# Seven half-width products instead of eight in 27 of 66 gate/up pairs, their weight sums made by adding transfers

## The reference

```python
FFN_DIM = D_FF = 2816                     # 22 features of 128
def conv_ffn(x, ln_g, up_w, conv_w, conv_b, down_w):          # blocks s = 0 and 1
    u = causal_dwconv(rms_norm(x, ln_g) @ up_w, conv_w, conv_b)     # three taps along the sequence
    gate, up = u[..., :FFN_DIM], u[..., FFN_DIM:]
    return (jax.nn.silu(gate) * up) @ down_w
def swiglu(xn, w_gate, w_up, w_down):                         # block s = 2
    return (jax.nn.silu(xn @ w_gate) * (xn @ w_up)) @ w_down
```

## Time and profile before

| | |
|---|---|
| median of 3 runs | 2398.46 us (2397.93 to 2400.35) |
| the profiled execution | 2399.27 us, span 2397.5 us |
| TensorE busy | 2371.2 us of the span |
| VectorE, ScalarE, GpSimd busy | 1484.8, 1086.1, 357.9 us |
| granted TensorE clock, mean | 0.998 |
| third block's gate and up, first to second down projection | about 2044 to 2330 us |
| read from memory | 215.87 MB |

### The profile page before, as it was taken

How to read it: one execution, slowest core, us unless ns; L and a number is a source line. 1 busy time by engine, 2 the same in 40 slices (tenths; PEclk the granted TensorE clock), 3 DMA queues, 4 the chain that set the end, 5 groups by cost and what they waited for, 6 DMA issues and landing times.

```text
span 2397.5 us, 30764 instructions
## 1 busy us (share of the span) xinstructions
PE 2371.2 (99%) x11952; PEld 1944.2 (81%) x11952; DVE 1484.8 (62%) x2356; ACT 1086.1 (45%) x1878; POOL 357.9 (15%) x286
## 2 busy tenths in 40 slices
PE   8999999999999999999999999999999999999999
PEld 6677878888888877788888877787788878898987
DVE  6778776763666777766456547534655445873763
ACT  6654554442445677644234334324443334442433
POOL 0252252210111000122011100001210001100001
PEclk9999999999999999999999999999999999999999
DMA  4532223223223221232332332231234332233232
GB/s 164 109 93 79 80 70 99 97 86 108 97 83 120 75 76 49 73 108 92 93 106 87 91 131 84 71 102 57 72 123 136 115 106 79 81 105 99 95 97 89
DMA packets 74847, 226.24 MB, mean 94 GB/s; under 512 B 8144, under 2 KB 12368, under 8 KB 74576
## 3 DMA queue, kind: packets, MB, share of 16 engines
q1 hardware_dynamic: 70272, 215.90, 28.1%
q10 hardware_dynamic: 4432, 8.39, 2.0%
HBM read 215.87 MB, written 8.39 MB: 94 GB/s over the span
## 4 chain that ended last, share of the span: by engine, by line
PE 60%; DVE 1%; ACT 0%; issue 0%; DMA 0%; POOL 0%; POOLq 0%; DVEq 0%; ACTq 0%; SPq 0%
PE bank L1272 59%; PE bank L1276 1%; DVE t L2230 1%; DVE t L2233 1%; ACT t L1715 0%; DVE t L2241 0%; DMA t<-in_w 0%; POOL t L2877 0%; ACT t L1718 0%; ACT L1718 0%; DVE t L2237 0%; DVE t L2798 0%; POOLq L3100 0%; DVEq L3100 0%; DVE t L2644 0%
## 5 line engine op out<-in xcount | busy, mean ns | idle before, releaser
L1272 PE MATMUL bank<-t 128*128 128x512 f32 (+5 forms) x11526 | 2346.4, 369 | 19.1 <-DVE t L2233 7.9
L1272 PEld LDWEIGHTS bank<-t 128*128 128x128 f32 (+2 forms) x11526 | 1901.0, 186 | 433.3 <-issue 80.1
L1715 ACT ACTIVATE t<-t 128x1024 fp32r<-128x1024 f32 (+5 forms) x676 | 564.0, 847 | 564.6 <-PE bank L1272 276.6
L2230 DVE TENSOR_TENSOR t<-t 128x1024 fp32r<-128x1024 f32 (+7 forms) x774 | 687.3, 901 | 202.9 <-ACT t L1715 192.4
L1718 ACT ACTIVATE t<-t 128x512 f32<-128x512 f32 (+6 forms) x610 | 367.5, 616 | 455.8 <-DVE t L2230 307.1
L2877 POOL TENSOR_TENSOR t<-t 128x512 f32<-128x512 f32 (+4 forms) x206 | 316.3, 1542 | 1551.9 <-ACT t L1718 559.7
L2230 DVE TENSOR_TENSOR t<-bank,t 128x512 f32<-128x512 f32 (+4 forms) x434 | 279.2, 648 | 425.2 <-PE bank L1272 414.7
L2233 DVE SCALAR_TENSOR_TENSOR t<-t 128x512 f32<-128x512 f32 (+5 forms) x536 | 386.6, 733 | 102.3 <-ACT t L1718 63.8
L1715 ACT ACTIVATE t<-bank 128x512 f32<-128x512 f32 (+4 forms) x184 | 84.7, 477 | 205.4 <-PE bank L1276 146.9
L2880 POOL TENSOR_SCALAR t<-t 128x128 f32<-128x128 f32 (+3 forms) x64 | 40.9, 645 | 478.6 <-ACT t L1715 247.6
L2233 DVE SCALAR_TENSOR_TENSOR t<-bank,t 128x512 f32<-128x512 f32 x56 | 38.5, 688 | 68.8 <-PE bank L1272 68.8
(11 more groups left out here) (30 smaller groups left out, 53.0 us busy)
## 6 DMA issues: line engine op xcount, KB each, us to landing
t<-in_w SPq DMA_DIRECT2D x304, 512.0 KB, 3.4
t<-in_w SPq DMA_DIRECT2D x48, 384.0 KB, 3.0
t<-in_w SPq DMA_DIRECT2D x56, 320.0 KB, 3.0
t<-in_w SPq DMA_DIRECT2D x28, 256.0 KB, 2.8
tab<-t ACTq DMA_DIRECT2D x1, 2560.0 KB
t<-in_x SPq DMA_DIRECT2D x8, 256.0 KB, 5.0
t<-tab SPq DMA_DIRECT2D x8, 256.0 KB, 3.7
spill<-t ACTq DMA_DIRECT2D x1, 2048.0 KB, 8.3
```

The costliest lines, as they stand in the source:

```text
L1272: return eng.matmul(out, lhs, rhs, start=start, stop=stop, skip_group_check=loose)
L1715: return eng.activation(out, in_, ACT.Copy, scale=scale)
L2230: return eng.tensor_tensor(out, a, b, o)
```

## The change

- Quads in all three feed-forward blocks: f = 9, 12, 14, 16, 18, 20 in blocks 0 and 1, and f = 4, 6 to 10, 12 to 20 in block 2. There rows of quads follow each other without an ordinary feature between them.
- The order of the products is p1, p5, p6, p3, p7, p2, p4, and the units are other ones: unit 0 (one half only) for p1, unit 1 (s12) for p5 and p6, unit 2 (s34) for p3 and p7, unit 3 for p2 and p4.
- The weights of a quad are one region in memory: gate low, up low, up high, gate high (four chunks of 512 columns each). Of it, SyncE loads a first quarter (256 KB) and the last half (512 KB) into raws, and three quarters (768 KB, `base`) into a buffer `sums`. GpSimd issues two transfers that add to what is there: the second and third quarter of the region onto the first two of `sums` (`add1`, 512 KB), then the first quarter of `sums` onto its third (`add2`, 256 KB). VectorE makes one sum (`add3`, 512 columns) into `sum4`. The four VectorE sums of before are gone.
- There are two `sums` buffers, used in turn; the second lies in the scratch of the norms and of the tees.
- `SUM_AGES` says how many ticks before the quad base, add1, add2 and add3 are issued. s34 is split and cut in two halves, since they lie in two tensors.
- In blocks 0 and 1 the quad's gate and up go through the convolution; its ticks are longer there.
- `cut_age` stays 2 within a quad (before: 1 for one unit).

```diff
-QUADS = (4, 5, 7, 8, 10, 12, 13, 15, 16, 18, 19)
-PRODUCTS = ("p1", "p2", "p6", "p5", "p7", "p3", "p4")
+QUADS = {0: (9, 12, 14, 16, 18, 20), 1: (9, 12, 14, 16, 18, 20), 2: (4, 6, 7, 8, 9, 10, 12, 13, 14, 15, 16, 17, 18, 19, 20)}
+QUAD_LIST = [(s, f) for s in range(3) for f in QUADS[s]]
+SUM_AGES = ((19, 15, 9, 3), (19, 15, 9, 3), (12, 9, 5, 1))
+PRODUCTS = ("p1", "p5", "p6", "p3", "p7", "p2", "p4")
+QUAD_HALF = {"p1": (0, 0), "p5": (1, 0), "p6": (1, 1), "p7": (2, 0), "p3": (2, 1), "p4": (3, 0), "p2": (3, 1)}
...
-        self.loads += [(gate, 0, DC, gate_c + f * P, P), (up, 0, DC, up_c + f * P, P)]
+        region = self.region((gate, 0, 4, gate_c + f * P, P), (up, 0, 4, up_c + f * P, P),
+                             (up, 4, 4, up_c + f * P, P), (gate, 4, 4, gate_c + f * P, P))
+        first = self.load(region, 0, S)
+        last = self.load(region, 2 * S, UNIT)
+        sources = (("raw", first, S), ("s12", (s, f), UNIT), ("s34", (s, f), UNIT), ("raw", last, UNIT))
         for i, product in enumerate(PRODUCTS):
-            if i % 2 == 0:
-                age, self.cut_age = self.cut_age, 1 if i == 4 else self.cut_age
-                u = self.ring(sources[i // 2])
-                self.cut_age = age
-                g.units.append(u)
+            if QUAD_HALF[product][0] == len(g.units):
+                g.units.append(self.ring(sources[len(g.units)]))
...
-        self.start("sum1", f, t - 5)
-        self.start("sum2", f, t - 3)
+        for name, age in zip(("base", "add1", "add2", "add3"), SUM_AGES[s]):
+            self.start(name, (s, f), t - age)
...
     def source(self, u):
+        if kind == "s12":
+            return [(0, n, self.sums(r)[:, S:3 * S])]
+        return [(0, S, self.sums(r)[:, 0:S]), (S, n, self.buf.sum4[:, :])]
...
     # ScalarE, quads: p1 copied at age 1, p5 at 2, p6 at 3 (before: p1 1, p6 3, p5 4); blocks 0 and 1 also:
+        for kind, age in (("ga", 7), ("up", 8)):
+            for s, f in at("quad", T - age):
+                func(ACT.Identity, buf.fv[n % 6][:, :], buf.fu[n % 3][:, 2:S + 2], pc(f"fcb{s}", ft),
+                     pc(f"fcw{s}", 3 * ft)).then_inc(*sig["tap0"].up((kind, s, f)))
...
     # VectorE, quads: bank d (p3) added at age 4, p7 at 5, bank a (p2) and the gate row at 6, the up row at 7
+        for sf in at("add3", T):
+            w.wait_ge(*K.loaded(last))
+            w.wait_ge(*K.added(sf, 1))
+            tt(buf.sum4[:, :], K.sums(sf)[:, 2 * S:3 * S], buf.raws[last % N_W][:, S:UNIT], ADD).then_inc(*sig["sum"].up(sf))
...
     # GpSimd
+    def adds(T):
+        for sf in at("add1", T):
+            w.wait_ge(*K.based(sf))
+            eng.dma_start(K.sums(sf)[:, 0:UNIT], K.region(region)[:, S:3 * S], accum_op=ADD).then_inc(
+                *sig.added[i][0].up())
+        for sf in at("add2", T):
+            w.wait_ge(*K.added(sf, 0))
+            eng.dma_start(K.sums(sf)[:, 2 * S:3 * S], K.sums(sf)[:, 0:S], accum_op=ADD).then_inc(*sig.added[i][1].up())
...
     # SyncE
+    def base(sf):
+        if before:
+            w.wait_ge(*sig["cut"].at(plan.quad_units[before][4]))
+        eng.dma_start(K.sums(sf)[:, 0:3 * S], K.region(region)[:, 0:3 * S]).then_inc(*sig.base[i].up())
```

More of the change, by code:

```diff
@@ L528, in ffn @@
         late = 5 if s < 2 else 2
[L529 to L531 removed]
+        apart = 4 if s == 2 else 12
+        for k in range(4 if QUADS[s] else 0):
+            self.once("tees", (s, k), lambda k=k: self.past("rms", src, 3) and (
+                k == 0 or self.past("tees", (s, k - 1), apart)))
         self.start("ffn", s)
@@ L2530, in quads @@
+        for s, f in at("quad", T - 6):
             vg, _ = K.quad_rows(f)
[L2531 to L2537 removed]
@@ L2551, in quads @@
-        for f in at("quad", T - 10):
-            src, i = h_of(2, f)
-            hi, lo = buf.operand(src, i)
-            w.wait_ge(*sig["hi"].at(src, i))
-            stt(lo, K.quad_rows(f)[1][:, :], -1.0, hi.bitcast(F), MUL, SUB).then_inc(*sig["lo"].up(src, i))
+            row = K.rms_row(FFN_IN[s])
+            w.wait_ge(*full(("gu", s, f, "a")))
+            tt(vg[:, 0:H2], K.of(("gu", s, f, "a"))[:, 0:H2], vg[:, 0:H2], ADD).then_inc(*leave(("gu", s, f, "a")))
+            w.wait_ge(*empty(("rb", FFN_IN[s])))
@@ new lines, in fu_free, with taps @@
+    def fu_free(n, s):
+        if n >= 3:
+            w.wait_ge(*sig["tap"].at(("ga" if (n - 3) % 2 == 0 else "up", s, (n - 3) // 2), 2))
+    def taps(key):
+        kind, s, f = key
+        n = 2 * f + (kind == "up")
+        ft = f + FFC * (kind == "up")
+        v, ub = buf.fv[n % 6], buf.fu[n % 3]
+        for k in (1, 2):
+            w.wait_ge(*(sig["tap0"].at(key) if k == 1 else sig["tap"].at(key, 1)))
+            stt(v[:, :], ub[:, 2 + k:S + 2 + k], pc(f"fcw{s}", 3 * ft + k), v[:, :], MUL, ADD).then_inc(
+                *sig["tap"].up(key, k))
@@ L3042, in sync_program @@
                 load(plan.units[u][1] + N_W)
+        for sf in at("base", T):
+            base(sf)
         for h in at("tb", T):
```

412 lines of the change are left out of this document (242 added, 170 removed).

## The result

The changed kernel takes 2480.8 us, the median of four runs (2478.7 to 2481.6), against 2398.9 for the kernel before, measured beside it: a ratio of 1.034 [1.0322, 1.0357]. It is slower by 82 us, where 17 were forecast. The sign was right; the size was not, and it lies outside the forecast range.

The account below looks back on a forecast made before the run. Bound: TensorE's columns plus its waits. Columns -12.8, old waits -2.8, late cuts (13 + 0.5) + (2.8 + 0.25 + 13.2), adding transfers +3: +17.2 on 2398.46, so 2416 us; range 2388 to 2440, the forecast's own 2408 to 2424.

Parts of the forecast that it names:

- the quad's worth of 0.80 us: TensorE's columns: each quad saves 0.80 us where nothing waits; sixteen more quads give -12.8 us.
- The wait at a joint: Third block, quad behind a quad: p5 waits 1.06, say 1.1 us, for VectorE's cut, twelve times, 13.2 us.
- The wait before p3: Quads behind ordinary features: unit 2's cut late by 1.3 us ten times (blocks 0, 1), 1.4 us twice (third block).
- Those terms: All forecast waits for late cuts, at joints and behind ordinary features or down projections: 29.75 us over 27 quads.
- the adding transfers: Chain base, add1, add2 of each quad: 10.2 to 16.4 us, taken as 13.3; costs 3 us in all.
- 3 us for the three: Third block, f = 4, 6 and 12: sums late by 1.0 us each; 0 at 10.2, 12 at 16.4.
- hidden at 13.3: Rows of quads: base issued 15.1 us ahead, so a 13.3 us chain costs nothing; at 16.4, 0.6 more a quad.
- The lead: Time by which the third block's base is issued ahead: 13.3 us at f = 4, 6, 12; 15.1 us in rows.
- The forecast's own formula, (chain + 7.2) / 2: Time per quad in a row when the chain exceeds its lead; 11.8 us for a 16.4 us chain.
- Rival 3: Adding transfers become the bound in the third block, at 16.4 us a chain: 2432 us; chance 18%.
- some 0.1 us more each time: Unit 2's split and cut, now on two halves instead of one piece, each take some 0.1 us longer.
- GpSimd's own multiplies wait behind its transfers by a few us at most, four ticks before they are needed.: GpSimd's queue: multiplies delayed a few us behind adding transfers, with four ticks to spare; no cost was added.

Follow-up runs that it names:

- e1: The changed kernel without GpSimd's two adding transfers (add1, add2), so its weight sums are wrong: 2430.2 us.
- e8: The changed kernel with the third block's base issued two ticks earlier (14 instead of 12): 2449.7 us.
- e10: The changed kernel without add2, the second adding transfer of each quad; base and add1 stay: 2439.8 us.
- e7: The changed kernel with ten spaced quads in block 2, base 19 ticks ahead, and the multiply before quads of blocks 0 and 1 on VectorE: 2415.4 us.
- e4: The changed kernel with the multiply of the feature ahead of a quad moved from GpSimd to VectorE in blocks 0 and 1: 2465.7 us.
- e3: The changed kernel with quads only in the third block (all 15), none in blocks 0 and 1: 2462.3 us.
- e5: The changed kernel with the old order of products and units, all 27 quads and the adding transfers kept: 2471.5 us.
- e11: Spaced-quad, old-order kernel (2399.8 us) with third-block multiplies before quads on VectorE and p7 waiting only for its half of the cut: 2389.6 us.
- e12: Spaced-quad, old-order kernel (2399.8 us) with the multiply of the feature before a quad on VectorE in the third block too: 2394.6 us.
- e9: Spaced-quad, old-order kernel (2399.8 us) with unit 2's cut a tick earlier, ahead of the taps, and third-block multiplies before quads on VectorE: 2399.1 us.

## Why the prediction was right in sign and wrong in size

**Right, as the runs showed.** The bound (TensorE's columns plus its waits), the quad's worth of 0.80 us and the sum as a method: it closes within 2.5 us in twelve of thirteen kernels. The wait at a joint, forecast 1.06, is 1.08 in e1, e8 and e10, and in those joints of the changed kernel that no transfer holds (0.53 in e7, where add3 stands two ticks earlier). The wait before p3, forecast 1.3 in blocks 0 and 1 and 1.4 in the third, is 1.33 (e4) and 1.2 to 1.4 (e1). f = 12 was put at 0.25 and is 0.21. SyncE issues a row's base at 7.3 us of the quad two before by the forecast, at 7.7 by the trace where that quad did not wait. Those terms came to 29.75 us; the runs have 15.1 (e4, blocks 0 and 1) and 16.1 (e1, third block) for them.

**The step that failed: the adding transfers.** "The chain is 10.2 to 16.4 us; I take the middle, 13.3", and so "3 us for the three" at f = 4, 6 and 12 and "hidden at 13.3" in the rows. Measured, this term is 48 us in the third block (64.3 to 16.1, e1): 21.6 at f = 4, 6 and 12, and 26.6 at the joints. The 15 chains of the third block took 14.5 to 21.3 us, 17.5 on the mean.

The bounds were drawn from plain transfers of the earlier trace rows. The base, put at 4.0, took 4.4 to 7.9 us, 5.1 in the median; add1, 3.4 to 6.8 by the bounds, took 5.1 to 7.2, 5.4 in the median; add2, 2.8 to 5.6 by the bounds, took 3.3 to 7.8, 4.1 in the median. Missing were the 0.3 and 0.5 us from one link's landing to GpSimd's issue of the next. In blocks 0 and 1, where no second chain runs beside the first, the chain took 15.8 us on the mean. So by the means, 2.5 of the missing 4.2 us were the links' own length and the gaps, and 1.7 came with the third block, where in a row of quads the last link of one chain runs beside the first of the next (there the base took 6.0 us on the mean, 5.0 in blocks 0 and 1; add2 took 7.0 to 7.8 at three joints). The lead was wrong too at the starts of two rows: 9.7 us at f = 4 and 11.5 at f = 6 where 13.3 was forecast (13.8 at f = 12). In the rows it was right: 14.8 to 16.0 us at the joints that waited, against 15.1.

A quad that waits long gives the next chain a longer lead, so long and short joints take turns, and the mean spacing from f = 13 to 20 is (2389.46 - 2294.49) / 7 = 13.6 us, where 11.2 was forecast. The forecast's own formula, (chain + 7.2) / 2, gives 12.5 with the 17.7 us that the chains of these eight quads took on the mean. The remaining 1.1 us a quad (the split and cut behind the landing, and the half-clock stretches, are candidates) was not taken apart. Rival 3 had the right mechanism, and a chain too short for its price: 2432.

**A size within a right mechanism: the wait before p3.** 2.4 us, not 1.3, in ten quads: 10.7 us (e4). For a cut in two halves the forecast gave "some 0.1 us more each time". But the multiply comes between the halves, and the second takes 1.07 us more. The cut of the earlier trace rows had been priced with a multiply beside it, and had not suffered, since it was one instruction and came first (2.20 us for the multiply, in the earlier trace rows too).

**A sentence that the traces contradict.** "GpSimd's own multiplies wait behind its transfers by a few us at most, four ticks before they are needed." They are needed sooner. At f = 4 of the changed kernel a multiply left the queue at 2096.16, behind an add1 issued at 2095.50 that had waited for its base. ScalarE's next step came at 2097.81, released by it, and TensorE stood idle 1.15 us before the quad, where e1 has no gap (timelines of GpSimd, ScalarE and TensorE):

```profile
2096.16 1.62 POOL L2972 TENSOR_TENSOR t<-t 128x512 f32<-128x512 f32 x1
...
2097.81 1.15 ACT L1764 ACTIVATE t<-t 128x512 fp32r<-128x512 f32 x2 [8.17 <-POOL t L2972]
...
2099.91 1.67 PE L1314 MATMUL bank<-t 128*128 128x256 f32 x12 [1.15 <-DVE t L2298]
```

In e7 the same cost 5 us at f = 18. The 48 us that e1 took away hold both, the late sums and this.

**A term that was missing: the clock.** The forecast let TensorE wait at full speed. After many of its waits of 2 us and more the granted clock was 0.50 for 3.4 us or longer; the changed kernel's matmuls are busy 26.7 us longer than their columns (2385.1 against 2371.2 - 12.8). Some 9 of that is in blocks 0 and 1 and went with the waits in e4; 14.5 is in the third block and went in e1. The waits of 1.1 to 1.4 us that I had forecast bring none: e1 has no such stretch in the third block, e4 none in blocks 0 and 1.

In the forecast's units: -12.8 - 3.4 + 29.8 (as forecast) + 48 (transfers, with their clock) + 19.5 (multiply, with its clock) = +81.

**Open.** Which of its neighbours makes add2 take 7.8 us instead of 4.1 was not measured; nor why the third block waits 5 to 6 us more when blocks 0 and 1 are quicker or have no quads (e4, e3), nor which of several equal waits brings a half-clock stretch.

## What to carry to other kernels

A chain of dependent transfers that is issued at a steady rhythm must be priced with its neighbours running and with the gaps between its links (here 17.5 us, 15.8 without a second chain beside it, 13.3 forecast), and against the rhythm itself: if the chain is longer than its lead, the periods stretch, and trimming other waits gave nothing back (e5). What stands behind such a transfer in the same queue waits with it. If an instruction is divided, ask what another engine can put between its parts. Before an instruction is moved ahead in an in-order queue, ask whether the reader needs all of what it waits for: a semaphore for the half that p7 reads gave 5 us (e11 against e12), and moving the cut instead gave nothing (e9 is 4.5 us slower than e12). And a wait of TensorE costs more than its length once it is long enough for the clock to fall (1.5 us more a time in blocks 0 and 1).
